# Depthwise taps of a mixer as matmuls with diagonals, and its first product in separate passes

## What is computed

```python
xn = rms_norm(h, g_mix_pre); z = xn @ w_in            # w_in cut in a, b, q, k, v, f, h, sb, c, p
u = a * sigmoid(b)                                    # 256 channels
u = causal_depthwise_conv(u, w_dw)                    # 31 taps for each channel
y_conf = silu(layer_norm(u, ln_g, ln_b)) @ w_pw
y_att  = forgetting_attention(q, k, v, f + b_forget)  # log_sigmoid(f) summed over the tokens
y_sc   = sb * causal_depthwise_conv(c * h, w_sc)      # 3 taps
y_pool = multiscale_pool(p, w_pool, pool_scale)
h = h + rms_norm(concat(y_conf, y_att, y_sc, y_pool) @ w_out, g_mix_post)
```

## Time and profile before

| | us |
|---|---|
| median of 3 runs | 1040.36 (1037.11 to 1040.70) |
| the profiled execution's own time | 1036.83 |
| its span, first to last instruction | 1035.0 |
| TensorE busy in the span | 965.6 |
| VectorE busy | 704.4 |
| ScalarE busy | 505.6 |
| GpSimd busy | 63.7 |
| mean granted TensorE clock | 0.981 |

### The profile page before, as it was taken

How to read it: one execution, slowest core, us unless ns; L and a number is a source line. 1 busy time by engine, 2 the same in 40 slices (tenths; PEclk the granted TensorE clock), 3 DMA queues, 4 the chain that set the end, 5 groups by cost and what they waited for, 6 DMA issues and landing times.

```text
span 1035.0 us, 13510 instructions
## 1 busy us (share of the span) xinstructions
PE 965.6 (93%) x5540; PEld 842.9 (81%) x5540; DVE 704.4 (68%) x936; ACT 505.6 (49%) x669; POOL 63.7 (6%) x89
## 2 busy tenths in 40 slices
PE   5989899999999798878999999989999899999997
PEld 5888697888887587666998888868989779888886
DVE  4799576666657876663677666656979876766664
ACT  4845554444446545564553443447655344434441
POOL 4200000000010100000000000010113100000000
PEclk9989999999999999889999999999999999999999
DMA  9554346565655354211566565646431346565631
GB/s 321 183 165 131 112 132 225 183 213 173 198 168 181 96 174 169 83 41 41 164 203 208 197 198 174 199 131 214 125 122 42 122 130 202 190 197 179 201 122 41
DMA packets 106190, 164.40 MB, mean 159 GB/s; under 512 B 2816, under 2 KB 82784, under 8 KB 106000
## 3 DMA queue, kind: packets, MB, share of 16 engines
q1 hardware_dynamic: 104688, 158.25, 47.5%
q0 software_dynamic: 1440, 5.28, 1.4%
HBM read 162.47 MB, written 1.05 MB: 158 GB/s over the span
## 4 chain that ended last, share of the span: by engine, by line
PE 71%; DVE 17%; ACT 6%; issue 4%; DMA 2%; POOL 1%; DVEq 0%; POOLq 0%; ACTq 0%
PE ps L380 69%; DVE wl L1659 6%; ACT wh L1113 2%; DVE SC L1760 2%; PE ps L388 2%; DMA raw<-in_w_in 1%; DVE xhl L1664 1%; DVE xf L1668 1%; DVE st L2057 1%; ACT junk L1101 1%; POOL st L2400 1%; ACT SC L1426 1%; DVE rows L2243 0%; ACT xhl L1124 0%; DMA h<-in_x 0%
## 5 line engine op out<-in xcount | busy, mean ns | idle before, releaser
L1659 DVE TENSOR_TENSOR wl<-raw,wh 128x2048 fp32r<-128x2048 f32 (+2 forms) x150 | 339.3, 2264 | 177.1 <-ACT wh L1113 176.8
L1113 ACT ACTIVATE wh<-raw 128x2048 fp32r<-128x2048 f32 (+2 forms) x150 | 282.0, 1884 | 169.1 <-PE ps L380 148.0
L380 PE MATMUL ps<-wh,xhl 128*128 128x512 f32 (+3 forms) x1000 | 257.9, 349 | 30.7 <-DVE wl L1659 11.6
L380 PE MATMUL ps<-xhl,wh 128*128 128x512 f32 (+1 forms) x1248 | 281.9, 352 | 4.4 <-DVE wl L1772 4.4
L380 PEld LDWEIGHTS ps<-xhl,wh 128*128 128x128 f32 x1248 | 216.4, 191 | 31.9 <-issue 5.6
L380 PEld LDWEIGHTS ps<-wh,xhl 128*128 128x128 f32 x1000 | 175.6, 196 | 54.7 <-DVE wl L1659 18.4
L380 PE MATMUL ps<-xhl,wl 128*128 128x256 f32 x1008 | 175.7, 283 | 0.0
L380 PE MATMUL ps<-wl,xhl 128*128 128x512 f32 (+3 forms) x500 | 171.7, 343 | 0.0
L380 PEld LDWEIGHTS ps<-xhl,wl 128*128 128x128 f32 x1008 | 151.6, 192 | 7.5
L380 PE MATMUL ps<-wh,fh 128*128 128x512 f32 x304 | 119.0, 391 | 1.8 <-DVE fl L1910 1.5
L380 PE MATMUL ps<-wh,fl 128*128 128x512 f32 x304 | 118.7, 390 | 0.0
(11 more groups left out here) (266 smaller groups left out, 823.2 us busy)
## 6 DMA issues: line engine op xcount, KB each, us to landing
raw<-in_ffn_gate SPq DMA_DIRECT2D x22, 1024.0 KB, 5.4
raw<-in_ffn_up SPq DMA_DIRECT2D x22, 1024.0 KB, 5.3
raw<-in_ffn_down SPq DMA_DIRECT2D x22, 1024.0 KB, 4.9
raw<-in_w_up SPq DMA_DIRECT2D x16, 1024.0 KB, 5.6
raw<-in_w_down SPq DMA_DIRECT2D x16, 1024.0 KB, 4.9
raw<-in_s_w_in SPq DMA_DIRECT2D x14, 1024.0 KB, 5.5
raw<-in_w_in SPq DMA_DIRECT2D x9, 1024.0 KB, 7.3
raw<-in_a_w_in SPq DMA_DIRECT2D x6, 1024.0 KB, 5.1
```

The costliest lines, as they stand in the source:

```text
L380: return e.matmul(o, a, b, start=start, stop=stop, skip_group_check=True)
L1113: e.activation(high_of(i), raw_of(i), ACT.Copy).then_inc(*up("act_high", i))
L1659: e.tensor_tensor(low_of(i), raw_of(i), high_of(i).bitcast(F32), ALU.subtract).then_inc(*up("dve_lo", i))
```

## The change

- The ring, `tap` on ACT and the sums on POOL go. ACT writes 18 diagonal matrices instead (128x128, identity times the weights of one tap), right behind the high half of slot 2 and ahead of those of slots 3 and 4.
- PE multiplies these 18 diagonals by 18 shifted views of tile 1 of `upad`, summed in bank `ps[3]`, in full float32, between the products q and k. DVE's tap 18 of tile 1 adds the bank; DVE then does taps 18 to 30 of this tile.
- `dve_glu` is done in two halves, tile 1 first. The first product goes pass by pass, both tiles in each pass, in banks `ps[4]` and `ps[2]`, with a wait ahead of each pass only for what that pass reads.
- In `softplus`, used twice, exp(-log) on ACT takes the place of the reciprocal on DVE.
- `highs(5)` and `lows(5)` stand ahead of the forget chain, `lows(6)` in it; the DVE taps are dealt out anew, `mix_low(3)` moves ahead of `forget_max(2)`, and `lows(12)` behind the centring.

The diff, without the lists of step names (they gain `act_diag` and `pe_conf_taps`):

```diff
@@ -22,7 +22,7 @@
 SCN = 11136
 LEVELS = [64, 32, 16, 8, 4, 2, 1]
 TAPS = 31
-BEGUN = 10
+DIAG = 18
 
 
 C_ID, C_MA, C_MT, C_ONE, C_SEL, C_ROPE = 0, 128, 256, 384, 512, 1536
@@ -199,7 +199,7 @@
         ft = hsf[:, 0:1024].rearrange("p (a b) -> p a b", a=4)
         Pf = hsf[:, 0:1536].rearrange("p (a b) -> p a b", a=4)
         PTf = fh_f[:, 0:1152].rearrange("p (a b) -> p a b", a=3)
-        tap_ring = fl_f[:, 0:1536].rearrange("p (a b) -> p a b", a=6)
+        diag = [fl_f[:, 128 * i:128 * i + 128] for i in range(12)] + [junk[:, 128 * i:128 * i + 128] for i in range(2, 8)]
 
 
         rb = SC[:, 0:1024].rearrange("p (a b) -> p a b", a=2)
@@ -490,13 +490,19 @@
                 e.wait_ge(*at("dma_ident"))
                 norm_turn(0, 0)
                 norm_turn(0, 1)
-                e.wait_ge(*at("dve_xl", 0, 1, 1))
+                e.wait_ge(*at("act_xh", 0, 1, 1))
                 wH, wL = weight(S["a"])
-                for t in range(2):
-                    e.wait_ge(*(halves_ready(S["a"]) if t else at("dve_first_low")))
-                    c = slice(128 * t, 128 * t + 128)
-                    for k in range(8):
-                        d = mm3(ps[4][:, 256 * t:256 * t + 256], wH[:, k, c], wL[:, k, c], xh[:, k, :], xl[:, k, :], k == 0, k == 7)
+                for n, (w, x) in enumerate(((wH, xh), (wH, xl), (wL, xh))):
+                    for t in range(2):
+                        if n == 0:
+                            e.wait_ge(*(at("act_high", 0) if t else at("act_first_high")))
+                        elif n == 2:
+                            e.wait_ge(*(halves_ready(S["a"]) if t else at("dve_first_low")))
+                        elif t == 0:
+                            e.wait_ge(*at("dve_xl", 0, 1, 1))
+                        for k in range(8):
+                            d = mm(ps[(4, 2)[t]][:, 0:256], w[:, k, 128 * t:128 * t + 128], x[:, k, :], n == 0 and k == 0,
+                                   n == 2 and k == 7)
                 d.then_inc(*up("pe_slot", S["a"]))
                 feat(S["b"], ps[5])
                 e.wait_ge(*at("dma_wf", 1))
@@ -504,11 +510,17 @@
                     d = mm(ps[6][0:36, 0:256], wf[:, k, :], xf[:, k, :], k == 0, k == 7)
                 d.then_inc(*up("pe_forget"))
                 feat(S["q"], ps[7])
+                e.wait_ge(*at("act_diag", DIAG - 1))
+                e.wait_ge(*at("dve_glu", 1))
+                for k in range(DIAG):
+                    d = mm(ps[3][:, 0:256], diag[k], upad[:, 1, k:k + 256], k == 0, k == DIAG - 1)
+                d.then_inc(*up("pe_conf_taps"))
                 feat(S["k"], ps[0])
                 for tb in range(2):
                     tok(S["v"], [(ps[1][:, 256 * tb:256 * tb + 256], slice(0, 256))], tb)
                 for tb in range(2):
                     tok(S["p"], [(ps[2][:, 256 * tb:256 * tb + 256], slice(0, 256))], tb)
+                e.wait_ge(*at("dve_tap", 1, DIAG))
                 feat(S["h"], ps[3])
 
                 e.wait_ge(*at("dma_band"))
@@ -516,7 +528,7 @@
                 for t in range(2):
                     o = ps[(5, 4)[t]]
                     if t == 1:
-                        e.wait_ge(*at("dve_glu"))
+                        e.wait_ge(*at("dve_glu", 0))
                     for i in range(2):
                         for tb in range(2):
                             d = mm(o[:, 256 * i:256 * i + 256], pv[:, tb, 128 * t:128 * t + 128], band[:, 2 * t + i, tb, :],
@@ -1149,15 +1161,9 @@
                 e.wait_ge(*at("dve_softplus", who, "1+u"))
                 e.wait_ge(*at("act_square", *squares[-1]))
                 e.activation(l, w, ACT.Ln).then_inc(*up("act_softplus", who, "log"))
-
-            def tap(k):
-
-                if k == 0:
-                    e.wait_ge(*at("dve_glu"))
-                if k >= 7:
-                    e.wait_ge(*at("pool_tap", k - 6))
-                e.activation(cacc[:, 1, :] if k == 0 else tap_ring[:, k % 6, :], upad[:, 1, k:k + 256], ACT.Identity,
-                             scale=P("dw", TAPS + k)).then_inc(*up("act_tap", k))
+                e.wait_ge(*at("act_softplus", who, "log"))
+                e.wait_ge(*at("dve_softplus", who, "kept"))
+                e.activation(w, l, ACT.Exp, scale=-1.0).then_inc(*up("act_softplus", who, "inverse"))
 
             def first_mixer():
                 norm_squares(0, 0)
@@ -1172,6 +1178,11 @@
                     x, y = (z.rearrange("p (k n) -> p k n", k=8)[:, :, 128 * t:128 * t + 128] for z in (raw_of(0), high_of(0)))
                     e.activation(y, x, ACT.Copy).then_inc(*(up("act_high", 0) if t else up("act_first_high")))
                 high[0] = 1
+                highs(2)
+                e.wait_ge(*at("dma_ident"))
+                e.wait_ge(*at("act_square", *squares[-1]))
+                for k in range(DIAG):
+                    e.activation(diag[k], C(C_ID), ACT.Identity, scale=P("dw", TAPS + k)).then_inc(*up("act_diag", k))
                 highs(4)
                 e.wait_ge(*at("dma_ident"))
                 e.wait_ge(*at("dma_cst"))
@@ -1179,19 +1190,15 @@
                     e.activation(o[:, :], C(c), ACT.Copy).then_inc(*up("act_masks", i))
                 e.wait_ge(*at("pe_slot", S["b"]))
                 e.activation(sg, ps[5][:, :], ACT.Sigmoid).then_inc(*up("act_sigmoid"))
-                for k in range(5):
-                    tap(k)
+                highs(5)
                 R = slice(0, 36)
                 softplus("forget", *(ft[R, i, :] for i in range(4)), junk[R, 0:256])
-                highs(5)
                 e.wait_ge(*at("pool_zero", 6))
                 e.wait_ge(*at("pe_slot", S["q"]))
                 for i in range(2):
                     r = slice(64 * i, 64 * i + 64)
                     e.activation(qm.rearrange("p (t i) n -> p t i n", i=2)[r, :, i, :],
                                  ps[7][r, :].rearrange("p (t n) -> p t n", t=2), ACT.Copy, scale=0.125).then_inc(*up("act_q", i))
-                for k in range(5, BEGUN):
-                    tap(k)
                 highs(6)
                 e.wait_ge(*at("pe_slot", S["k"]))
                 e.activation(kT, ps[0][:, :].rearrange("p (t n) -> p t n", t=2), ACT.Copy).then_inc(*up("act_k"))
@@ -1735,9 +1742,8 @@
                 e.tensor_scalar(a, w, -1.0, None, ALU.add).then_inc(*up("dve_softplus", who, "kept"))
                 e.wait_ge(*at("dve_softplus", who, "kept"))
                 e.tensor_tensor(a, u, a, ALU.subtract).then_inc(*up("dve_softplus", who, "lost"))
-                e.wait_ge(*at("act_softplus", who, "log"))
-                e.reciprocal(w, w).then_inc(*up("dve_softplus", who, "inverse"))
-                e.wait_ge(*at("dve_softplus", who, "inverse"))
+                e.wait_ge(*at("dve_softplus", who, "lost"))
+                e.wait_ge(*at("act_softplus", who, "inverse"))
                 e.tensor_tensor(a, a, w, ALU.mult).then_inc(*up("dve_softplus", who, "mend"))
                 e.wait_ge(*at("dve_softplus", who, "mend"))
                 e.tensor_tensor(a, a, l, ALU.add).then_inc(*up("dve_softplus", who, "mended"))
@@ -1753,10 +1759,13 @@
                     for k in range(a, b):
                         x, w = upad[:, t, k:k + 256], P("dw", TAPS * t + k)
                         if (t, k) == (0, 0):
-                            e.wait_ge(*at("dve_glu"))
+                            e.wait_ge(*at("dve_glu", 0))
                             e.tensor_scalar(o, x, w, None, ALU.mult).then_inc(*up("dve_tap", t, k))
+                        elif (t, k) == (1, DIAG):
+                            e.wait_ge(*at("pe_conf_taps"))
+                            e.scalar_tensor_tensor(o, x, w, ps[3][:, 0:256], ALU.mult, ALU.add).then_inc(*up("dve_tap", t, k))
                         else:
-                            e.wait_ge(*(at("pool_tap", BEGUN - 1) if (t, k) == (1, BEGUN) else at("dve_tap", t, k - 1)))
+                            e.wait_ge(*at("dve_tap", t, k - 1))
                             e.scalar_tensor_tensor(o, x, w, o, ALU.mult, ALU.add).then_inc(*up("dve_tap", t, k))
 
                 norm_rows(0, 0)
@@ -1774,15 +1783,19 @@
                 lows(4)
                 e.wait_ge(*at("act_sigmoid"))
                 e.wait_ge(*at("pool_zero", 2))
-                e.tensor_tensor(upad[:, :, 30:286], ps[4][:, :].rearrange("p (t n) -> p t n", t=2),
-                                sg.rearrange("p (t n) -> p t n", t=2), ALU.mult).then_inc(*up("dve_glu"))
-                taps(0, 0, 5)
+                for t in (1, 0):
+                    e.tensor_tensor(upad[:, t, 30:286], ps[(4, 2)[t]][:, 0:256], sg[:, 256 * t:256 * t + 256], ALU.mult).then_inc(
+                        *up("dve_glu", t))
+                lows(5)
+                taps(0, 0, 4)
+                taps(1, DIAG, DIAG + 1)
                 R, F4, G4 = slice(0, 36), slice(0, 4), slice(32, 36)
                 fx, fa, fu, fw = (ft[R, i, :] for i in range(4))
                 e.wait_ge(*at("pe_forget"))
```

(38 more changed lines are left out.)

## The result

The changed kernel takes 1042.51 us (median of 20 runs, 1037.47 to 1045.32) against 1040.05 (20 runs, 1036.34 to 1041.57) for the kernel before: a ratio of **1.0031, interval 1.0019 to 1.0044**, 3.2 us slower. The profiled execution took 1045.12 us, its span is 1043.3 us.

What follows compares the result with a forecast made beforehand. In the first mixers the bound was when DVE reaches its last tap. +2.7 (glu) +6.4 (waits) -7.85 (work off DVE) = +1.3, with smaller terms +1.9 us, put on the median: 1042.3 us, range 1035.5 to 1047.

Steps and rivals of the forecast that it cites:

- rival A: PE cools in the hole ahead of the taps and runs them at half clock: slower, 1044.9 us, chance 0.15.
- First product worth nothing: PE's first product starts 2.0 us earlier, but what follows q waits for the later glu: no gain.
- Diagonals: 18 scaled copies on ACT at 0.30 us each, 5.4 us, partly covered by idle time: sigmoid +2.7 us.
- PE's taps: 36 PE passes after glu at 0.21 us each: 7.6 us, done at 47.3, bounds 6.9 and 8.1.
- 3.3 is shorter than both: PE's 3.3 us hole ahead of the taps is shorter than holes of 5.0 and 3.75 us followed by slow clock.
- Waits on DVE: New DVE waits in the first mixers: 0.9 + 2.1 + 1.7 + 1.65 us, together +6.4 us.
- Work off DVE: Eight taps, the reciprocal and contention with POOL leave DVE, less 0.15 us for split glu: -7.85 us.
- Exp for the reciprocal: In softplus, Exp 0.42 us plus table load 1.28 replace a 1.75 us reciprocal; the forget chain keeps its length.
- Recurrent softplus: The second softplus gets one more load and an Exp, 1.7 us: zero cost, 1.1 if the cover fails.
- Rival B: PE was the bound and everything that fills or shortens it counts: faster, 1037.8 us, chance 0.12.
- Rival C: Exp needs no table load and the diagonals cost 0.20 us each: 1038.5 us, chance 0.12.
- Rival D: DVE's work is not taken away, contention gives back nothing (+2.1 us): 1044.4 us, chance 0.06.

Runs made afterwards that it cites:

- e1: The changed kernel with its first product back in the old order, tile by tile from the low half on; ratio 1.0017 to the kernel before.
- e10: e6 with the first product back in the old order, tile by tile from the low half on; ratio 0.9973 to the kernel before.
- e4: The changed kernel with the 18 diagonals written ahead of the high half of slot 2; ratio 0.9999 to the kernel before.
- e7: The changed kernel with 16 more matmuls on PE between product q and the tap matmuls, sums overwritten; ratio 1.0004 to the kernel before.
- e9: e7 with nine additions that feed nothing put back on POOL; ratio 1.0046 to the kernel before.
- e2: The changed kernel with the reciprocal back on DVE in both softplus places, no second Exp; ratio 1.0018 to the kernel before.
- e8: The changed kernel run once more without any edit, beside other follow-up kernels; ratio 1.0029 to the kernel before.
- e3: The changed kernel with DVE's tap 18 of tile 1 moved behind the forget chain; ratio 1.0016 to the kernel before.
- e5: The changed kernel with the edits of e3 and e4 together; ratio 0.9963 to the kernel before.
- e6: e5 with the reciprocal back on DVE and mix_low(3) back behind forget_max(2) and its taps; ratio 0.9961 to the kernel before.

## Why the prediction was right, and where it was not

*The sign and the place held, the size only in part.* The forecast was 1042.3 us and the median measured 1042.51. That the two are 0.2 us apart is in part luck: the sum said +1.9 us where the ratio says +3.2, and the base of 1040.36 was 0.3 above the later median of 20 runs. The loss is in the order of the work around the taps, as the sum had it, and not in the amount. But the missing part of it is rival A, whose own figure, 1044.9, was too high in part because it took a stretch of 5.2 us where 3.4 came.

- *First product worth nothing:* this was right, shown by e1. Worse, it fed the hole; by itself it pays only once PE bounds (e10).
- *Diagonals:* 0.30 us each was right (0.29). The sigmoid ended at 39.0 (39.2 said), and the taps started at 39.66 (39.7 said). That this was the dearest part, and that its cover lay one line higher, e4 showed.
- *PE's taps:* 7.6 us at full clock was right (7.7 in e1 and e7). What failed is the step "3.3 is shorter than both", by which the hole of 3.3 us would keep the clock. It was made rival A, at 0.15, and A came in: 3.4 us at half clock, 1.7 us more. The forecast x of 47.9 was 48.37 in e1 and 47.50 in e7, at full clock, and 49.79 with the half clock. So of the loss at the mark the sum lacked mainly this term: 1.9 + 1.7 = 3.6, measured 4.0 and 3.8.
- *Waits on DVE:* 0.9, 1.7 and 1.65 us were right (0.95, 2.48 less the old 0.67, and 1.65). The wait for the taps was 4.49 instead of 2.1: 1.7 of it is the clock, the rest small shifts at both ends. The 0.1 us booked for the first tap that reads a bank had no row behind it, and that tap took 0.48 us, no more than its neighbours.
- *Work off DVE:* the least sure part was right where the forget chain lies: the scan took 0.68 us and the bias rows 0.88, shown as POOL's doing by e9. The 0.7 us of two faster taps was booked as gained; behind those taps stands the wait for PE, which takes it up again.
- *Exp for the reciprocal:* the load stands between Ln and Exp, at 54.19. By the rule of the Trainium skill, ScalarE: Activation LUTs, "Table sets: the hidden batching unit", Ln and then Exp need one load; this trace does not agree, 1.28 us stand between them. The sum booked the 1.75 us as saved and 1.7 + 1.65 us of waits as the price, 1.6 us lost; e2 shows 1.7.
- *Recurrent softplus:* zero was right. From the kernel before to e8, x of that block moved from 717.36 to 721.03 us and the scan behind it from 734.35 to 738.03, 3.7 us both.
- *Rival B*, PE as the bound, fell for the changed kernel: with the first product 2 us later nothing came later (e1), and the chain of the changed kernel from 36 to 112 us is PE for 23% only. It holds where the wait for the taps is gone: PE is the bound in e3, level with DVE in e5, and the bound in e6 and e10.
- *Rival C:* neither half came in; the load was there, and a diagonal took 0.29 us and not 0.20. *Rival D* did not come in either: DVE's rows beside the idle POOL were faster.

## What to carry to other kernels

Work taken off the bounding engine is gained only where that engine does not meet a new wait: look at which instruction waits for the new producer and what stands behind it in program order, and put it last among what is ready. Put new helper work into a wait that the trace shows (here ACT's 9.5 us for slot 2) and not one line behind it; these two one-line moves turned +0.31% into -0.37%. An earlier start on an engine that does not bind only lengthens its next hole, and a hole on PE that costs nothing itself can make the work behind it slow (1.7 us here).

## What the runs showed of the hardware

The hole that costs the clock is shorter than I took it. Ahead of the taps, holes of 2.13 to 3.31 us were followed by half clock in all four profiles that had one (both of the changed kernel, e2, e3), holes of 0.76 to 1.06 in none (e1, e4, e5), nor was e7's filled one. The stretch lasted 3.4 us, or 6.8 in e3.

The length of the hole does not decide alone. Ahead of the product with slot 9 most of these kernels have a hole too, 1.95 us in e1 and 3.37 in e9. PE of the two, each with the clock behind the hole:

```profile
95.14 0.70 PE L380 MATMUL ps<-wh,xhl 128*128 128x512 f32 x2 [1.95 <-issue]
96.20:99.60 3.40, 3.40 (x10) 0.52 0.90 281
```

```profile
95.75 0.70 PE L380 MATMUL ps<-wh,xhl 128*128 128x512 f32 x2 [3.37 <-issue]
95.75:98.75 3.00, 3.00 (x13) 1.00 0.71 180
```

The shorter hole was followed by half clock and the longer one was not. A hole of 1.95 to 1.97 us at this place was followed by half clock in e1 and e4 and by full clock in e7, e8 and the first profile. What else decides is not shown.

The stretches of half clock later in the program vary with no change in the code. The first profile of the changed kernel has a span of 1043.3 us at a mean clock of 0.977, and e8, the same kernel, 1038.8 us at 0.983. At the mark they are 0.2 us apart, at the end 4.5. In two places, from 129 and from 364 us on, the first stayed at half clock twice as long. The second place, first kernel, then e8:

```profile
364.30:371.10 6.80, 5.16 (x13) 0.51 0.32 101
```

```profile
364.50:367.90 3.40, 2.93 (x7) 0.54 0.52 153
```

So one profile's span says little of a change of 0.3%; the mark in the stage and the ratio over many runs do.
